# Sixteen of the 22 chunks of each down projection by seven products instead of eight (Strassen), in a two-block fp32 kernel on one Trainium2 core

## The reference, cut to what matters

```python
D_FF = 2816
def swiglu(x, w_gate, w_up, w_down):
    return (jax.nn.silu(x @ w_gate) * (x @ w_up)) @ w_down

for l in range(DEPTH):                                   # DEPTH = 2
    x = layer_norm(ALPHA * x + 0.5 * swiglu(x, ...ffn1...), ln_g[l, 0], ln_b[l, 0])
    ...                                                  # a mixer, layer_norm
    x = layer_norm(ALPHA * x + 0.5 * swiglu(x, ...ffn2...), ln_g[l, 2], ln_b[l, 2])
```

## Time and profile before

| | |
|---|---|
| median of 3 runs | 2991.75 us (2991.3 to 2992.64) |
| profiled execution | 2993.77 us, span 2991.8 us, mean granted clock 0.991 |
| PE busy | 2898.5 us (97%) |
| PEld, DVE, ACT, POOL busy | 2415.7, 1377.7, 1024.3, 83.7 us |
| matmuls of the down projections (L404 to L406, `h_hi`, `h_lo`) | 3 x 704 |
| `w_lo` on DVE (L1508) | 234 times, mean 2289 ns |
| `w_hi` on ACT (L998) | 234 times, mean 1896 ns |

### The profile page before, as it was taken

The page is one execution under the profiler, slowest core; times in us unless marked ns, Lnnn a source line. Parts: engine busy times, 40 slices in busy tenths (PEclk is TensorE's granted clock), DMA queues, the critical chain, the costliest instruction groups (busy, mean ns, idle before and its releaser), DMA issues.

```text
span 2991.8 us, 33948 instructions
## 1 busy us (share of the span) xinstructions
PE 2898.5 (97%) x14593; PEld 2415.7 (81%) x14593; DVE 1377.7 (46%) x1931; ACT 1024.3 (34%) x1360; POOL 83.7 (3%) x91
## 2 busy tenths in 40 slices
PE   7999998999999999999999999999999999999998
PEld 7888877887888778888876888888888886788887
...
DMA packets 41957, 280.01 MB, mean 94 GB/s; under 512 B 5636, under 2 KB 5826, under 8 KB 10064
## 3 DMA queue, kind: packets, MB, share of 16 engines
...
## 4 chain that ended last, share of the span: by engine, by line
PE 90%; DVE 5%; ACT 2%; issue 1%; DMA 1%; ACTq 0%; DVEq 0%
PE G L392 16%; PE G L394 16%; PE G L393 16%; PE G L404 11%; PE G L406 11%; PE G L405 11%; DVE w_lo L1508 1%; PE A L894 1%; PE A L579 1%; PE A L916 1%; PE A L675 1%; PE A L904 1%; PE A L692 1%; PE A L662 1%; DMA x<-in_x 1%
## 5 line engine op out<-in xcount | busy, mean ns | idle before, releaser
L1508 DVE TENSOR_TENSOR w_lo<-raw,w_hi 128x2048 fp32r<-128x2048 f32 (+1 forms) x234 | 535.7, 2289 | 805.3 <-ACT w_hi L998 804.8
L392 PE MATMUL G<-xT_hi,w_hi 128*128 128x512 f32 (+1 forms) x2368 | 881.4, 372 | 14.9 <-DVE x L2067 4.8
L394 PE MATMUL G<-xT_hi,w_lo 128*128 128x512 f32 (+1 forms) x2368 | 870.7, 368 | 0.0
L393 PE MATMUL G<-xT_lo,w_hi 128*128 128x512 f32 (+1 forms) x2368 | 870.2, 367 | 0.0
L998 ACT ACTIVATE w_hi<-raw 128x2048 fp32r<-128x2048 f32 (+1 forms) x234 | 443.8, 1896 | 954.4 <-PE G L406 507.2
L392 PEld LDWEIGHTS G<-xT_hi,w_hi 128*128 128x128 f32 x2368 | 449.5, 190 | 86.8 <-DVE xT_lo L1549 5.3
L394 PEld LDWEIGHTS G<-xT_hi,w_lo 128*128 128x128 f32 x2368 | 449.3, 190 | 73.3
L393 PEld LDWEIGHTS G<-xT_lo,w_hi 128*128 128x128 f32 x2368 | 449.9, 190 | 69.0
L404 PE MATMUL G<-w_hi,h_hi 128*128 128x512 f32 x704 | 274.7, 390 | 1.0 <-DVE w_lo L1508 1.0
L406 PE MATMUL G<-w_hi,h_lo 128*128 128x512 f32 x704 | 274.0, 389 | 0.0
L405 PE MATMUL G<-w_lo,h_hi 128*128 128x512 f32 x704 | 273.9, 389 | 0.0
...
## 6 DMA issues: line engine op xcount, KB each, us to landing
...
```

What stands on the lines that cost most here:

```text
L392: mm(o, a, hi[:, c, at:at + n], start=start and own_start, stop=False, **k)
L393: mm(o, a, lo[:, c, at:at + n], start=False, stop=False, **k)
L394: return mm(o, wl[:, col:col + P], hi[:, c, at:at + n], start=False, stop=stop, **k)
L1508: tt(w_lo[:, s, 0:nk, :], raw[:, r, 0:nk, :], w_hi[:, s, 0:nk, :].bitcast(F32), ALU.subtract).then_inc(lo_done, 1)
```

## The change

Each feed-forward part is now three parts: 4 units and a down projection of 8 chunks by seven products, the same again, and 3 units with two down projections of 6 chunks (a block of four and one of two) as before. The first two halve tokens, contraction (even and odd chunks) and output columns; each of the seven products is 256 tokens by 4 chunks by 512 columns, 24 matmuls. Products share PSUM banks, two banks each in turn (0 and 1, then 2 and 3), and some go on summing in their banks; DVE adds the banks to the right quarter of `x` after each (`read_product`). The left operands are h11, h12, h22 and four sums of the quarters of h: seven tiles of 256 tokens in `hs` (high and low) for each unit, written in three groups, [0:1], [1:3] and [3:7]. The right operands are the four quarters of the weight block and sums of them: two sums on DVE in the last unit ahead of the products (`raw[1] -= raw[0]`, `raw2[0] -= raw[1]`), two on GpSimd (`raw[0] = raw2[0] - raw[0]` and `raw2[1] -= raw2[0]`), each 128x2048. SP loads the quarters with rows of 2 KB into `raw` and a new pair `raw2`, and one of them twice (`alternate`). ACT's first step for the second product's weights stands between the copies of the last unit's h. GpSimd's clearing of `shift_t` moves behind the products.

```diff
-FF_HALVES = ((6, (4, 4, 4)), (5, (4, 4, 2)))
+SUMMED = 2
+LAST_DOWN = (4, 2)
+FF_HALVES = ((4, (4, 4)), (4, (4, 4)), (3, LAST_DOWN))
+FF_PARTS = tuple(units for units, _ in FF_HALVES)
+PRODUCTS = 7
+LEFT = (0, 1, 4, 3, 5, 6, 2)
+QUARTER = ((0, 0), (0, 0), (0, 1), (1, 1), (1, 1), (0, 1), (1, 0))
...
+            def alternate(place, b, odd, signals):
+                for o in range(2):
+                    sp.dma_start(place[:, 2 * o:2 * o + 2, :],
+                                 stream[b + o:b + o + 1].rearrange("o p (k e n) -> (o p) k e n", e=2, n=BC)[:, :, odd, :]
+                                 ).then_inc(signals[o], 16)
...
+                    first = Q.split
+                    alternate(raw2[:, 0], b + 2, 1, (raw2_in[0], raw2_in[0]))
+                    alternate(raw2[:, 1], b, 1, (raw2_in[1], raw2_in[1]))
+                    slot_free()
+                    alternate(raw[:, 0], b, 0, (half_in[0], raw_in[0]))
+                    taken(first + 4)
+                    slot_free()
+                    alternate(raw[:, 1], b + 2, 0, (half_in[1], raw_in[1]))
+                    taken(first + 3)
+                    sp.wait_ge(lo_done, first + 2 + 3)
+                    sp.wait_ge(S["w_sum"], 4 * (parts_before + n) + 4)
+                    alternate(raw2[:, 0], b + 2, 1, (raw2_in[0], raw2_in[0]))
+                    Q.split += PRODUCTS
+                    b += 4
...
-            FF_ORDER = ((0, 0, 0, 4), (0, 1, 0, 4), (0, 2, 0, 4), (0, 3, 0, 4), (1, 0, 0, 4), (2, 0, 0, 2), (1, 1, 0, 4),
-                        (2, 1, 0, 2), (1, 2, 0, 4), (1, 3, 0, 2), (1, 3, 2, 4), (2, 2, 0, 2), (2, 3, 0, 2))
+            FF_ORDER = ((0, 0, 0, 4), (1, 0, 0, 2), (0, 1, 0, 4), (1, 1, 0, 2), (0, 2, 0, 4), (0, 3, 0, 4),
+                        (1, 2, 0, 2), (1, 3, 0, 2))
...
+            def products(units):
+                for k in range(PRODUCTS):
+                    s, a = (Pos.off + Pos.turn) % 2, 2 * (k % 2)
+                    pe.wait_ge(lo_done, 2 * Pos.pair + Pos.off + 3)
+                    for i in range(2):
+                        if k < 2:
+                            pe.wait_ge(g_free[a + i], Pos.ubase + Pos.u + 1)
+                        else:
+                            pe.wait_ge(S["st_read"], N.st + 2 * (k - 2) + i + 1)
+                        o = G[:, a + i, :]
+                        for u in range(units):
+                            if i == 0:
+                                pe.wait_ge(S["ff_lo"], N.ff + 3 * u + min(k, 2) + 1)
+                            hi, lo = (hs[:, u, part, LEFT[k], i * P:i * P + P] for part in range(2))
+                            new, end = u == 0 and k in (0, 1, 3), u == units - 1
+                            mm(o, hi, w_hi[:, s, u, :], start=new, stop=False, skip_group_check=True)
+                            mm(o, hi, w_lo[:, s, u, :], start=False, stop=False, skip_group_check=True)
+                            last = mm(o, lo, w_hi[:, s, u, :], start=False, stop=end, skip_group_check=True)
+                        last.then_inc(blk_used if i else S["st_done"], 1)
+                    Pos.off += 1
+                N.st += 2 * PRODUCTS
+                Pos.held.update({0: N.st - 1, 1: N.st, 2: N.st - 3, 3: N.st - 2})
...
-                        for i in range(2):
-                            act.wait_ge(g_free[2 + i], Pos.ubase + Pos.u + 2)
-                            fn(h_hi[:, 2 * u + i, :], work[:, 1024 + i * 512:1536 + i * 512],
+                        if n < SUMMED:
+                            act.wait_ge(g_free[2], Pos.ubase + Pos.u + 2)
+                            fn(hs[:, u, 0, 0, :], work[:, 1024:1280], ACT.Copy).then_inc(S["ff_hi"], 1)
+                            if before_products:
+                                act.wait_ge(raw2_in[1], 32 * (N.parts + 1))
+                                split_summed(raw2[:, 1])
+                            act.wait_ge(g_free[3], Pos.ubase + Pos.u + 2)
+                            fn(hs[:, u, 0, 1:3, :], work[:, 1536:2048].rearrange("p (a t) -> p a t", a=2),
                                ACT.Copy).then_inc(S["ff_hi"], 1)
-                        split()
+                            if before_products:
+                                act.wait_ge(S["w_sum"], 4 * N.parts + 2)
+                                split_summed(raw2[:, 0])
+                            N.sums += 1
+                            act.wait_ge(S["ff_sum"], N.sums)
+                            fn(hs[:, u, 0, 3:7, :], work[:, 0:1024].rearrange("p (a t) -> p a t", a=4),
+                               ACT.Copy).then_inc(S["ff_hi"], 1)
+                            N.ff += 3
...
+            def low_h(u, a, b, source):
+                N.ff += 1
+                dve.wait_ge(S["ff_hi"], N.ff)
+                tt(hs[:, u, 1, a:b, :], source.rearrange("p (a t) -> p a t", a=b - a), hs[:, u, 0, a:b, :].bitcast(F32),
+                   ALU.subtract).then_inc(S["ff_lo"], 1)
+            def sums_of_h(u):
+                dve.wait_ge(g_free[2], Pos.ubase + Pos.u + 2)
+                dve.wait_ge(g_free[3], Pos.ubase + Pos.u + 2)
+                h11, h21, h12, h22 = (work[:, 1024 + i * 256:1280 + i * 256] for i in range(4))
+                s1, s2, s3, s4 = (work[:, i * 256:i * 256 + 256] for i in range(4))
+                tt(s3, h11, h21, ALU.subtract)
+                link(tt(s1, h21, h22, ALU.add))
+                link(tt(s2, s1, h11, ALU.subtract))
+                tt(s4, h12, s2, ALU.subtract).then_inc(S["ff_sum"], 1)
+            def first_weight_sum():
+                first = 2 * Pos.pair + Pos.off - Pos.fewer
+                for half in range(2):
+                    dve.wait_ge(raw_in[half], (first // 2 + 1) * 16)
+                    dve.wait_ge(half_in[half], 16 * (N.parts + 1))
+                tt(raw[:, 1], raw[:, 1], raw[:, 0], ALU.subtract).then_inc(S["w_sum"], 1)
+            def second_weight_sum():
+                dve.wait_ge(raw2_in[0], 32 * (2 * N.parts + 1))
+                dve.wait_ge(S["w_sum"], 4 * N.parts + 1)
+                tt(raw2[:, 0], raw2[:, 0], raw[:, 1], ALU.subtract).then_inc(S["w_sum"], 1)
+            def read_product(k, n):
+                half, col = QUARTER[k]
+                for i in range(2):
+                    if i == 0:
+                        dve.wait_ge(S["st_done"], PRODUCTS * N.parts + k + 1)
+                    else:
+                        dve.wait_ge(blk_used, 2 * Pos.pair + Pos.end + k + (3 if k == 0 else 1))
+                    if k in (1, 4):
+                        dve.wait_ge(S["st_read"], 2 * (PRODUCTS * N.parts + k - 1) + i + 1)
+                    o = x[:, 2 * half + i, col * 512:col * 512 + 512]
+                    g = G[:, 2 * (k % 2) + i, :]
+                    if n == 0 and k in (0, 2, 3, 6):
+                        ins = stt(out=o, in0=o, scalar=2.0 * ALPHA, in1=g, op0=ALU.mult, op1=ALU.add)
+                    else:
+                        ins = tt(o, o, g, ALU.add)
+                    ins.then_inc(S["st_read"], 1)
...
+                for n, units in enumerate(FF_PARTS):
                     for u in range(units):
+                        before_products = n < SUMMED and u == units - 1
+                        if before_products:
+                            first_weight_sum()
                         split()
+                        if before_products:
+                            second_weight_sum()
                         for i in range(2):
                             done(2 + i)
 
                             ins = tt(work[:, 1024 + i * 512:1536 + i * 512], work[:, i * 512:i * 512 + 512],
                                      G[:, 2 + i, :], ALU.mult)
                             ins.then_inc(g_free[2 + i], 1)
-                        for i in range(2):
-                            N.ff += 1
-                            dve.wait_ge(S["ff_hi"], N.ff)
-                            tt(h_lo[:, 2 * u + i, :], work[:, 1024 + i * 512:1536 + i * 512],
-                               h_hi[:, 2 * u + i, :].bitcast(F32), ALU.subtract).then_inc(S["ff_lo"], 1)
+                            if n < SUMMED and i == 0:
+                                low_h(u, 0, 1, work[:, 1024:1280])
+                        if before_products:
+                            split_summed(raw2[:, 1])
+                            low_h(u, 1, 3, work[:, 1536:2048])
+                            sums_of_h(u)
+                            if n == 0 and before is not None:
+                                dve.wait_ge(S["x_res"], 4 * (before + 1))
+                            read_product(0, n)
+                            split_summed(raw2[:, 0])
+                            low_h(u, 3, 7, work[:, 0:1024])
...
+                        read_product(1, n)
+                        split_summed(raw[:, 1])
+                        read_product(2, n)
+                        split_summed(raw[:, 0])
+                        read_product(3, n)
...
+                    add_half(1.0, 0, True, (0,))()
```

(16 more changed lines are left out.)

273 lines of the change are left out of this document (182 added, 91 removed).

## The result

The changed kernel takes **3024.72 us** (median of four runs, 3023.24 to 3027.01), against 2992.19 us of the kernel before in the same comparison: ratio 1.0104, 95% interval 1.0092 to 1.0116. It is 1.0% slower. 3016 was forecast, with a range of 2963 to 3032. The profiled execution has a span of 3024.0 us, 32.2 more than before.

What follows compares the result with a forecast made beforehand. PE was taken as the bound, busy 2898.5 of 2991.8 us. Matmuls -43.5, first waits +12.8, second waits +34.4, clock +6.4, last down projections +14.0 gave +24.1 on the median 2991.75: 3016 us, range 2963 to 3032.

Steps and rivals of the forecast that it cites:

- What is removed: Eight groups of products, each 168 matmuls in place of 192: 43.5 us less PE time, all there is to win.
- GpSimd against DVE: GpSimd's 128x2048 sums and DVE instructions with two SBUF inputs exclude each other for whole instructions; a sum takes 4.8 us.
- The beginning of a group: At each group's start PE waits 1.6 us in the first product and 4.3 ahead of the third: 5.9 a group.
- The clock: Half clock on PE behind the 4.3 us gap in each group: 0.8 a group, +6.4 us (0 to 12).
- The last down projections: Halves of 6 chunks instead of 10 hide less: layer norms +11.6, program end +3.4, w_lo wait -1.0; +14.0 us (8 to 18).
- only the second sum: Rival: in each group only GpSimd's second sum meets DVE, third product 4.2 us late; +10.5, 3002 us; chance 0.15.
- GpSimd does not hold DVE off: Rival: GpSimd's long sums do not hold DVE, or not for their length; at most 1.6 a group, 2969 us; chance 0.18.
- All hidden: Rival: all waiting in the groups hidden, layer norms too, tails overestimated by half; -36.5, 2955 us; chance 0.09.
- Worse: Rival: GpSimd sums at 5.2 us and loads at 6.5 bring 7.8 a group, low clock 12; 3037 us; chance 0.08.

Runs made afterwards that it cites:

- the first experiment: Both of GpSimd's weight sums replaced by plain signals in the changed kernel, so two of seven products use wrong weights: 2962.1 us, ratio 0.9899 to the kernel before.

## Why the prediction held, point by point

**What is removed**: right. Without GpSimd's sums the groups are exactly as long as their matmuls, and 2962.1 is 43.5 under the kernel before plus 13.6 for the rest.

**GpSimd against DVE**: right in kind and close in size. 4.57 and about 4.5 net for a sum against my 4.8, inside the bounds of 4.2 to 5.2. The rule of the Trainium skill (SBUF — State Buffer, Who interferes with whom) held for an instruction of 4.57 us, where the earlier trace rows had shown 1.29, in both directions and for whole instructions. By the same section of the Trainium skill an instruction with at most one SBUF input is not held off; the trace agrees, as the multiplication with a PSUM input took its usual 0.68 us beside GpSimd's pieces. The Trainium skill's figure of 4497 ns for the sum (GPSIMD Engine Reference, Elementwise) is 0.07 under the measured 4.57.

**The beginning of a group**: right. I forecast the third product 16.8 us after the first; it starts after 16.7 to 17.8 in the eight groups. I had 1.6 for the first wait and 4.3 for the second, 5.9 together; they are 2.2 (17.3 in eight) and, where no low clock shortened it, 3.67, together 5.8. The first is longer and the second by the same amount shorter because low h11 is held until GpSimd ends at +4.0, not +3.1. What makes it late is the load of `raw[1]`: the first experiment's median of 6.2 us is over all 80 halves, but the one that DVE waits for was issued 13.3 us ahead of the group and took 5.7 (5.3 to 6.4), so it landed at -7.5, not at -8.6 (means of eight). In part it was luck that the third product was forecast so well: the load came 1.1 later, and GpSimd's two sums took 0.2 to 0.3 less each than assumed.

**The clock**: undersized, and this is the term that was off. I had 0.8 a group. A group costs 7.8 (62.3 in eight) where the waits alone are 5.8: 2.0 more, of which about 0.5 are two restarts and 1.5 the low clock behind the second wait. 8 x (7.8 - 6.7) = 8.8 us, and the kernel's 3024.7 lies 8.7 over 3016. The range held the time, but the term itself came to 16 us in eight groups, over the 12 that I gave as its upper bound. That a low clock behind the first wait costs nothing, I had not seen.

**The last down projections**: +14.0 forecast, +13.4 left over in the account. The tail is exact: the last tile's addition starts 3016.36, PE's last matmul starts 3012.59, and from there to the end of the span it is 11.4 us instead of 8.1, +3.3 (3.4 forecast). The tiles come 5.03 us apart as in the earlier trace rows:

```profile
3001.23 0.67 DVE L2218 TENSOR_TENSOR x<-x,G 128x512 f32<-128x512 f32 x1
...
3011.32 0.68 DVE L2218 TENSOR_TENSOR x<-x,G 128x512 f32<-128x512 f32 x1
3016.36 0.68 DVE L2218 TENSOR_TENSOR x<-x,G 128x512 f32<-128x512 f32 x1
```

PE's wait of 0.98 for `w_lo` in the last part is gone, as forecast.

Inside, the sum was near and the working in part wrong. The waits for the transposes are 2.50, 2.79 and 2.50, where I had 3.9, 1.4 and 3.9. With `bias` (first and third) the chain of ACT, split and tiles came as forecast: the transposes start 20.4 us after the half's start (S+20.5), but PE reaches their place at S+17.9 and not at S+16.6. Without `bias` the split ahead of the tiles waits for its load, which I had put at nothing, and they start at S+16.6 and not S+15.0:

```profile
1457.72 0.33 PE L545 MATMUL A<-ident,x 128*128 128x128 f32 x1 [2.50 <-ACT x L1171]
```

```profile
2034.77 1.92 ACT L1109 ACTIVATE w_hi<-raw 128x2048 fp32r<-128x2048 f32 x1 [5.48 <-DMA raw<-in_stream]
```

```profile
2036.72 2.29 DVE L1661 TENSOR_TENSOR w_lo<-raw,w_hi 128x2048 fp32r<-128x2048 f32 x1 [1.72 <-ACT w_hi L1109]
```

The later wait for `x` grew by 0.9 over the three places instead of 4.2. In all, the waits inside grew by 7.0 us where 11.6 were forecast. What closes the sum is the clock again, which I had given no share here: in each of the three layer norms a stretch of 3.4 us at the lower level, about 1.7 us each. That the two errors cancel is luck. The stretches behind the transposes in the second and third:

```profile
2047.00:2051.00 4.00, 4.00 (x20) 3.73 (x19) 0.99 (x2) 3.52 (x7) 0.00 (x0) 0.57 0.00 0
2427.00:2431.00 4.00, 4.00 (x19) 3.75 (x18) 1.18 (x2) 3.71 (x7) 0.36 (x1) 0.66 0.95 69
```

By the distances between the same instructions before and after, the three layer norms hold about 12.3 of the 13.4 us and the end of the program 2.2; places that the change does not touch make about -1.1, most of it the clock.

**The rivals**: "only the second sum" was run as a kernel, and costs 3006 and not 3002: the wait is 3.5 us, less than the 4.2 of that rival, but the clock falls behind it in six of eight groups. "GpSimd does not hold DVE off" (2969) falls with the two DVE instructions of 3.86 and 4.83 us; no run has the sums without the holding, and the kernel without the sums takes 2962. "All hidden" falls with the same rows, and with the 13.4 us of the rest. "Worse" had 7.8 us a group, the number that was measured, for another reason: its GpSimd sum of 5.2 us was 4.57, and of the 7.8 only 5.8 are waits.

**Left open**: what decides whether the clock falls, since it stayed up behind two waits of 3.5 us and fell behind one of 1.81. Nothing was tried on that.
